# One index in SyncE's loop over the attention heads: when the weight blocks are stored, against when the next head is loaded

## The reference

```python
q = (_rmsnorm(c_q, q_norm_g) @ w_uq).reshape(b, s, MLA_HEADS, MLA_NOPE + MLA_ROPE)
kv = (_rmsnorm(c_kv, kv_norm_g) @ w_ukv).reshape(b, s, MLA_HEADS, MLA_NOPE + MLA_V)
...
sc = (jnp.einsum('bqhd,bkhd->bhqk', qn_i, kn)
      + jnp.einsum('bqhr,bkr->bhqk', qr_i, kr)).astype(jnp.float32) * scale
a = jax.nn.softmax(sc, axis=-1).astype(v.dtype)
return jnp.einsum('bhqk,bkhd->bqhd', a, v)
...
x = x + jax.nn.sigmoid(x @ w_ple_gate[i]) * (p[i] @ w_ple[i])
```

## Time and profile before

| | us |
|---|---|
| median of 3 runs | 1996.65 |
| lowest and highest | 1993.53, 2000.44 |
| the profiled execution's own time | 1996.65 |
| its span on the core | 1994.9 |
| PE busy | 1921.7 (96%) |
| DVE, POOL, ACT busy | 1143.9, 761.8, 687.1 |

### The profile page before, as it was taken

How to read it: one execution, slowest core, us unless ns; L and a number is a source line. 1 busy time by engine, 2 the same in 40 slices (tenths; PEclk the granted TensorE clock), 3 DMA queues, 4 the chain that set the end, 5 groups by cost and what they waited for, 6 DMA issues and landing times. The chain is left out here.

```text
span 1994.9 us, 26356 instructions
## 1 busy us (share of the span) xinstructions
PE 1921.7 (96%) x9784; PEld 1603.8 (80%) x9784; DVE 1143.9 (57%) x1735; ACT 687.1 (34%) x1409; POOL 761.8 (38%) x538
## 2 busy tenths in 40 slices
PE   4999999999989999999989999999999999999999
PEld 3888888887889788788877888877898998788787
DVE  5599999826768317524754100175777776234775
ACT  6111212211578332212223111122677775323322
POOL 0111121122587544454533222133699851531101
PEclk8999999999999999999989999999999999999999
DMA  4202333443476556534320222286546332656734
GB/s 171 64 11 69 133 95 109 144 141 114 164 260 219 182 165 223 198 114 135 131 66 15 79 90 69 88 326 182 165 133 201 121 105 64 229 209 225 259 126 145
DMA packets 152242, 286.11 MB, mean 143 GB/s; under 512 B 31489, under 2 KB 70145, under 8 KB 152130
## 3 DMA queue, kind: packets, MB, share of 16 engines
q1 hardware_dynamic: 152130, 284.62, 43.0%
HBM read 181.61 MB, written 102.96 MB: 143 GB/s over the span
## 5 line engine op out<-in xcount | busy, mean ns | idle before, releaser
L593 DVE SCALAR_TENSOR_TENSOR ie_acc<-ie_u,ie_wconv,ie_acc 128x1551 f32<-128x1551 f32 x120 | 249.8, 2081 | 3.2
L191 POOL TENSOR_TENSOR w_lo_part<-w_raw,w_hi_part 128x1024 fp32r<-128x1024 f32 x24 | 66.3, 2763 | 335.0 <-ACT w_hi_part L183 335.0
L1598 PE MATMUL op_ps<-w_hi_part,rows_hi 128*128 128x512 f32 x384 | 157.1, 409 | 5.0 <-DVE rows_lo L1157 2.6
L173 POOL TENSOR_TENSOR w_hi_part<-w_raw,zero 128x1024 fp32r<-128x1024 f32 x48 | 92.8, 1933 | 173.7 <-DMA w_raw<-wall 171.9
L328 PE MATMUL ie_ps<-rows_hi,w_hi_part 128*128 128x512 f32 x384 | 153.1, 399 | 4.8 <-DVE w_lo_part L557 4.8
L1598 PE MATMUL op_ps<-w_hi_part,rows_lo 128*128 128x512 f32 x384 | 152.3, 397 | 0.0
L328 PE MATMUL ie_ps<-rows_hi,w_lo_part 128*128 128x512 f32 x384 | 152.1, 396 | 0.0
L1598 PE MATMUL op_ps<-w_lo_part,rows_hi 128*128 128x512 f32 x384 | 152.1, 396 | 0.0
L328 PE MATMUL ie_ps<-rows_lo,w_hi_part 128*128 128x512 f32 x384 | 151.1, 394 | 0.0
L2870 DVE TENSOR_TENSOR mla_pt_lo<-mla_ps_t,mla_pt_hi 128x512 fp32r<-128x512 f32 x160 | 108.9, 686 | 26.2 <-ACT mla_pt_hi L2839 25.1
L175 POOL TENSOR_TENSOR w_lo_part<-w_raw,w_hi_part 128x1024 fp32r<-128x1024 f32 x48 | 119.1, 2480 | 3.8
(11 more groups left out here) (291 smaller groups left out, 5088.6 us busy)
## 6 DMA issues: line engine op xcount, KB each, us to landing
w_raw<-wall SPq DMA_DIRECT2D x76, 512.0 KB, 4.6
op_in<-x SPq DMA_DIRECT2D x24, 512.0 KB, 4.5
x<-op_in SPq DMA_DIRECT2D x24, 512.0 KB, 3.0
weight_blocks<-w_hi_part SPq DMA_DIRECT2D x20, 512.0 KB, 4.9
w_hi_part<-weight_blocks SPq DMA_DIRECT2D x14, 512.0 KB, 6.8
w_lo_part<-weight_blocks SPq DMA_DIRECT2D x14, 512.0 KB, 6.7
pro_x<-x SPq DMA_DIRECT2D x12, 512.0 KB, 7.9
op_in<-attn SPq DMA_DIRECT2D x24, 256.0 KB, 3.1
```

Source lines behind the costliest of these rows:

```text
L173: pool.tensor_tensor(hi, raw, g.zero[:, 0:1].broadcast_to([P, QCOLS]), ALU.add).then_inc(g.w_hi, 1)
L593: dve.scalar_tensor_tensor(acc[:], ubuf[:, cc, s:s + CW], wconv[:, cc, s:s + 1], acc[:], ALU.mult, ALU.add).then_inc(taps, 1)
L1598: mm = pe.matmul(product_at(c * NT + t), g.XT[a][:, k, t * P:(t + 1) * P], w_at(g, name, m, k * HALF, HALF), start=k + a + m == 0, stop=k ...
```

## The change

In SP's loop, the chunks stored in the iteration of head h are those that `CHUNKS` gives for h, and no longer those that it gives for h-1. No other engine's instructions change, and SP issues the same DMAs in another order.

```diff
             for h in range(2, HEADS):
                 sp.wait_ge(ml.prepped, h * ml.PREPS)
                 ml.load(g, sp, h, slice(h * DH, (h + 1) * DH))
-                for i in CHUNKS.get(h - 1, []):
+                for i in CHUNKS.get(h, []):
                     wb.store(sp, i)
                 if h % 2:
                     pl.wait(sp, "normed", (h - 1) * NG)
```

## The result

| | before | changed |
|---|---|---|
| first comparison, median | 1997.82 us (4 runs) | 2028.65 us (4 runs) |
| its ratio, 95% interval | | 1.0157 [1.0131, 1.0183] |
| second comparison, median | 1998.08 us (17 runs) | 2021.95 us (5 runs) |
| its ratio, 95% interval | | 1.0135 [1.0107, 1.0163] |
| profiled execution, time and span | 1996.65, 1994.9 us | 2019.76, 2018.0 us |

A forecast was written before the change was run, and what follows sets the result against it. PE bounds the kernel in this stretch, with POOL a second chain nearly as long. POOL's chain overruns by 21.6 us, plus 1.7 for the clock: 1996.65 + 23.3 = 2020.0 us, range 2011 to 2031.

The forecast's parts named there:

- POOL's chain sets the starts of the heads: Heads 3 to 6: POOL's four turns take 165.6 us against PE's 140.5 plus 3.5 slack, so 21.6 us too long.
- Landing and issue: Loads of heads 3 to 6: issue 1.2 or 1.7 us, landing 8.0 behind a lo store, 10.2 with the attention store.
- the reverse case: A 0.5 MB store behind a 1.5 MB load takes 8.0 us in place of 2.6, read as 3.6 us per MB.
- The pause of 1.4 us a turn: POOL's wait for the first hi store while splitting chunks goes, leaving 17.4 us for four chunks, 13.1 for three.
- The clock: PE's granted clock falls after its waits; only the loss after the last, at head 6, counts: 1.7 us, bounds 0 to 3.4.
- The waits: PE waits for POOL 3.7 us at head 3, about 8 at head 4, 1 at head 5, 5 at head 6.
- The sum: Whole kernel: 21.6 us of POOL's chain plus 1.7 of clock, 23.3 us slower, 2020.0 us; chance 0.70.
- A: Loads of heads 3 to 6: stores in front cost nothing, each lands in 7.2 us; 2012.4 us, chance 0.12.
- C: Loads of heads 3 to 6 cost only by bytes, 6.2 us from the first issue; 2004.8 us, chance 0.04.
- B: Loads of heads 3 to 6 land as late as head 0's, 12.0 us; 2031.5 us, chance 0.10.
- D: Loads of heads 3 to 6, alone in the queue, land in 2.6 us; time stays at 1996.65 or falls slightly, chance 0.04.

## Why the prediction was right

The chain of steps held, and no step of it failed; two terms were sized too small, the chain's (by 1.0 us, mostly the loads behind the attention store) and the clock's (by 0.7). The terms came out as follows (from the first profile of the changed kernel).

- **POOL's chain sets the starts of the heads.** Forecast 42.2, 44.9, 37.9 and 40.6 us for its four turns, 165.6 together. Measured, from one head's operands being ready to the next one's: 42.0, 45.6, 38.4 and 40.9, 166.9. Less PE's 140.5 and the slack of 3.8 (head 2 ready at 1459.34, used at 1463.16) that is 22.6, forecast 21.6. With the clock's 2.4 it makes the 25.0 of the stretch.
- **Landing and issue.** Forecast 9.2 and 11.9 us; POOL idled 9.1 and 9.7, and 12.9 and 12.3. The two halves were divided wrongly, and the errors nearly cancel, which is luck. Behind a lo store the issue took 1.7 us, not 1.2, and the landing at head 3 7.3, not 8.0. Behind the attention store SP took 3.8 us from the end of POOL's last split to the issue of `ml_xv`, not 1.7, and the landing from there was 8.9, not 10.2, as the chain of waits of the changed kernel has it (start, us, what):

```profile
1516.22 2.41 POOL w_hi_part L1282
1522.46 8.89 DMA ml_xv<-mla_v
```

  The time that a load waits for the queue shows partly at the issuing engine (1.62 us for `ml_xq` at head 4 against 0.43 at head 3). That the sum was near may be because the reverse case that it was read from, a store behind a load, holds the whole delay; no run tests this.
- **The pause of 1.4 us a turn** went, as forecast.
- **The clock.** Forecast 1.7 us after the last wait, measured 2.4. Windows of 1 us of the changed kernel around the wait at head 6, columns as above:

```profile
1623.00:1624.00 1.00, 0.00 (x0) 0.00 (x0) 0.00 (x0) 0.00 (x0) 1.00 (x1) 1.00 0.00 0
1624.00:1625.00 1.00, 0.00 (x0) 0.00 (x0) 0.00 (x0) 0.00 (x0) 1.00 (x2) 0.83 0.00 0
...
1627.00:1628.00 1.00, 1.00 (x4) 0.81 (x3) 0.00 (x0) 0.00 (x0) 0.00 (x0) 0.50 0.99 141
...
1631.00:1632.00 1.00, 1.00 (x4) 0.82 (x4) 0.67 (x2) 0.86 (x2) 0.00 (x0) 0.75 0.88 158
1632.00:1633.00 1.00, 1.00 (x8) 0.82 (x8) 0.29 (x1) 0.00 (x0) 0.00 (x0) 1.00 1.26 149
```

  It fell to 1.2 GHz near 1624.7, inside the wait, and was back near 1631.5, 5.1 us after PE had begun again; in the earlier trace rows it was back about 4 us after PE's wait. The 1.7 was read from a wait of 3.1 us; the wait at head 6 was 5.5.
- **The waits**: forecast 3.7, 8, 1 and 5 us, measured 3.0, 8.7, 0.3 and 5.5.
- **The sum**: forecast 23.3 us. Measured 25.0 in the stretch and 23.1 for the profiled execution; that the last is so near is luck, since the rest of that execution happened to be 1.9 us shorter. The two comparisons give 31 and 27 by ratio, with intervals of 26 to 37 and 21 to 33: the forecast lies in the second and below the first. The forecast of 2020.0 us stands 8.6 below the first median. Of that, 1.7 are the terms above; for the rest no profile shows a place.

Of the rivals, A (the stores in front cost nothing) is refuted by the attention store: in front of the load it costs 2.4 us more than behind. C (only bytes) had 6.5 to 7 us of issue and landing together, and with the stores moved away POOL still waits near 9. B was too late by 1 to 4 us a head. D, the lone load that lands in 2.6, is refuted by the same 9 us. The Trainium skill's rule on the cost of a DMA issued by GpSimd ("DMA: Bandwidth & Descriptors", section "Anatomy of one DMA — SWDGE (gpsimd) path"), carried over to this load of SyncE, gave an estimate of 5.6 us from the first issue. With the lo stores moved behind it the whole idle time, issue included, was 8.5 to 9.5, so the trace disagrees with it for this load. Whether the part that moves in pieces of 256 B is the reason, no run shows.

## What to carry to other kernels

A load into a single buffer should be issued when the buffer comes free, ahead of anything on the same queue that waits for work of its consumer; moved behind it, the load's full 9 us went onto the helper engine's chain. What this costs is read by adding up the helper's turn and comparing it with the main engine's: one open load at a head with 9 us of slack cost nothing, four in a row at 38 to 46 us a turn against 35 cost 25 us. An engine that is busy 33 of 35 us beside the critical one is itself nearly critical, and its slack, not its share, says what it can take.

## What the runs showed of the hardware

- A store queued directly ahead of a load can show on the issuing engine as well. SP's issue of `ml_xq` took 0.3 us on an empty queue, 0.4 behind one lo store (but 1.68 once, at head 3 with three chunks a head), and 1.6 to 1.7 behind a lo store and the attention store. What set the one apart is not shown.
- After a wait of PE of 5.5 us the granted clock stayed at half for 5.1 us of new work, and that cost 2.4 us. Waits of 1.7 to 2.3 us, too, were each followed by a stretch at half that cost 1.7 to 1.8 us (with PE kept busy, head 3: 1.72; with the lo stores behind, heads 6 and 3: 1.81 and 2.33). Waits of 1.1 to 1.6 us, all at head 5, cost 0.2 us at most. With a wait of 2.35 us and 3.3 us of small matmuls ahead of it, the clock did not fall at all, in the one case there is.
